# Hybrid attention and feed-forward trunk on one core: the transpositions of the probabilities move inside the projection's matmuls

## What is computed

```python
for layer in range(DEPTH):                      # DEPTH = 2
    hn = rms_norm(h, norm_mix_g[layer])
    h = h + hybrid_mixer(hn, positions, w_in[layer], ..., w_out[layer], layer)
    hn = rms_norm(h, norm_ffn_g[layer])
    h = h + conv_glu_ffn(hn, w_up[layer], conv_ffn_w[layer], w_down[layer])
return rms_norm(h, final_g)
```

```python
a = softmax(q1 @ k1.T) - lam * softmax(q2 @ k2.T)     # causal, per block of 128 queries
o = a @ v                                             # then rms_norm over the head
```

## Time and profile before

| | |
|---|---|
| median of 3 runs | 2609.04 us (2607.76 to 2612.22) |
| the profiled execution | 2612.52 us, of which 2610.7 us are the span of its instructions |
| TensorE busy in the span | 2437.4 us (93%) |
| VectorE, ScalarE, GpSimd busy | 1522.6, 880.9 and 1192.4 us |
| attention with projections, first layer | about 84 to 459 us of the span |
| the same in the second layer | about 1364 to 1739 us |

### The profile page before, as it was taken

One profiled execution on the slowest core, in us unless ns is written; L12 is line 12 of the kernel. 1 busy time (PEld: TensorE's weight loads), 2 busy tenths in 40 slices (PEclk: granted clock), 3 DMA queues, 4 the chain that ended last, 5 costly groups with the idle time before them and its releaser, 6 DMA issues.

```text
span 2610.7 us, 30963 instructions
## 1 busy us (share of the span) xinstructions
PE 2437.4 (93%) x11478; PEld 2017.6 (77%) x11478; DVE 1522.6 (58%) x2161; ACT 880.9 (34%) x1667; POOL 1192.4 (46%) x786
## 2 busy tenths in 40 slices
PE   7799999797999999999989999979889999999996
PEld 6688888675788888888768888868658888888884
DVE  8544777637545555555575456774565555555546
ACT  3344444413322333332414344443232332222322
POOL 3111221347666666666421121131676666666663
PEclk9899999898999999999989999989989999999997
DMA  3000101320111111111210010112111111111111
GB/s 141 25 25 25 33 28 38 92 57 25 49 49 65 49 49 49 54 60 62 95 66 25 25 33 25 33 49 60 57 33 49 58 56 65 49 49 49 49 49 65
DMA packets 55749, 131.33 MB, mean 50 GB/s; under 512 B 4784, under 2 KB 24368, under 8 KB 55600
## 3 DMA queue, kind: packets, MB, share of 16 engines
q1 hardware_dynamic: 54016, 128.07, 15.0%
q10 hardware_dynamic: 1584, 1.28, 0.2%
HBM read 119.64 MB, written 9.44 MB: 49 GB/s over the span
## 4 chain that ended last, share of the span: by engine, by line
PE 69%; DVE 20%; ACT 4%; issue 3%; POOL 3%; DMA 1%; DVEq 0%; POOLq 0%; SPq 0%; ACTq 0%
PE ps L780 14%; PE ps L781 13%; PE ps L782 13%; PE ps L747 6%; PE ps L749 6%; PE ps L748 6%; PE ps L988 3%; DVE k_next L1790 3%; PE ps L975 2%; DVE h L1471 2%; PE ps L962 1%; PE ps L963 1%; ACT prob L1233 1%; DVE q_next L1446 1%; DVE h L1469 1%
## 5 line engine op out<-in xcount | busy, mean ns | idle before, releaser
L539 POOL CAST w_hi<-stage 128x1024 fp32r<-128x1024 f32 x68 | 70.7, 1040 | 859.4 <-PE ps L749 796.7
L747 PE MATMUL ps<-x_hi,w_hi 128*128 128x512 f32 x960 | 389.3, 406 | 11.3 <-POOLq L544 4.7
L574 POOL TENSOR_TENSOR w_lo<-more_stage,w_hi 128x512 fp32r<-128x512 f32 x202 | 293.7, 1454 | 209.8 <-ACT w_hi L1302 192.4
L574 POOL TENSOR_TENSOR w_lo<-stage,w_hi 128x512 fp32r<-128x512 f32 x194 | 281.4, 1451 | 214.2 <-ACT w_hi L1302 197.9
L749 PE MATMUL ps<-x_hi,w_lo 128*128 128x512 f32 x960 | 377.7, 393 | 0.0
L748 PE MATMUL ps<-x_lo,w_hi 128*128 128x512 f32 x960 | 376.7, 392 | 0.0
L1408 DVE TENSOR_TENSOR h<-ps,h 128x1024 f32<-128x1024 f32 x160 | 194.4, 1224 | 192.3 <-PE ps L782 189.0
L780 PE MATMUL ps<-T_hi,w_hi 128*128 128x512 f32 x704 | 282.0, 401 | 19.7 <-DVE T_lo L1674 6.5
L780 PE MATMUL ps<-mix,w_hi 128*128 128x512 f32 x704 | 279.3, 397 | 10.9 <-POOLq L577 5.8
L781 PE MATMUL ps<-T_lo,w_hi 128*128 128x512 f32 x704 | 279.6, 397 | 0.0
L782 PE MATMUL ps<-T_hi,w_lo 128*128 128x512 f32 x704 | 279.3, 397 | 0.0
(11 more groups left out here) (200 smaller groups left out, 4582.7 us busy)
## 6 DMA issues: line engine op xcount, KB each, us to landing
stage<-stream SPq DMA_DIRECT2D x112, 512.0 KB, 3.7
more_stage<-stream SPq DMA_DIRECT2D x68, 512.0 KB, 4.3
h<-x_t SPq DMA_DIRECT2D x16, 512.0 KB, 5.5
stage<-stream SPq DMA_DIRECT2D x18, 448.0 KB, 4.6
saved_h<-h SPq DMA_DIRECT2D x8, 512.0 KB, 4.8
h<-saved_h SPq DMA_DIRECT2D x8, 512.0 KB, 3.3
out_t<-h SPq DMA_DIRECT2D x16, 256.0 KB, 2.1
stage<-stream SPq DMA_DIRECT2D x18, 64.0 KB, 4.8
```

Source lines behind the costliest of these rows:

```text
L574: pool.tensor_tensor(block_of(w_lo, n), raw, block_of(w_hi, n).bitcast(f32), ALU.subtract)\
L747: pe.matmul(out, w_hi[:, s, w], hi, start=start, stop=False)
```

## The change

In units 0 to 4 the turn of the first group (with `turn_v` in step 0) is no longer issued ahead of the half projection but inside it, behind its third row (key 3 of `between`). The turn of the second group, where a step has one, is issued ahead of the eighth and last row (key 7) and no longer behind the projection. Unit 5 keeps its order. No instruction is added or taken away, and no other engine's list is touched.

```diff
                         if i < QB - 1:
                             scores(g + 1, i + 1)
-                        turn_group(g, i, dilated, layer, u, 0)
-                        if i == 0:
-
-                            pe.wait_ge(evac_done, first_half + PROJECTED_V[u])
-                            turn_v()
+
+                        def turn_first():
+                            turn_group(g, i, dilated, layer, u, 0)
+                            if i == 0:
+
+                                pe.wait_ge(evac_done, first_half + PROJECTED_V[u])
+                                turn_v()
+
+                        def turn_second():
+                            if len(todo) > 1:
+                                turn_group(g, i, dilated, layer, u, 1)
+
                         if u < FINAL:
                             if i % 2 == 0:
                                 n = next_tile()
-                            project_half(n, i % 2, PROJ + i % 2)
-                        elif i >= 2:
+                            project_half(n, i % 2, PROJ + i % 2, {3: turn_first, 7: turn_second})
+                        else:
+                            turn_first()
+                        if u == FINAL and i >= 2:
...
                         for m in range(len(todo)):
-                            if m + 1 < len(todo):
+                            if m + 1 < len(todo) and (m or u == FINAL):
                                 turn_group(g, i, dilated, layer, u, m + 1)
                             ended = attend_group(g, i, dilated, layer, u, m)
```

## The result

The changed kernel took 2617.4 us (median of 7 runs, 2612.88 to 2619.64), the kernel before 2610.53 us beside it (7 runs, 2607.76 to 2612.5). The ratio, estimated from all these runs, is 1.0022 (some 5.7 us), with a 95% interval of 1.0013 to 1.0032; the medians are 6.9 us apart. The kernel is slower by 0.2%, where I had forecast 0.4 us. 2617.4 us lies inside the range given, by 0.6 us. One of e1's twelve executions took 12132.71 us and is left out of every number here.

What follows compares the result with a forecast made beforehand. TensorE was taken as the bound, busy 93% of the span, standing 14 us a layer in the attention. The terms summed to +0.2 us a layer, +0.4 in all: 2609.4 us, range 2602 to 2618.

Steps and rivals of the forecast that it cites:

- Interleaving costs nothing: Half projection on TensorE: a turn moved inside it keeps its 0.11 us a transposition, with a surcharge of 0.
- The first rival: Each of 136 turns moved inside the projection costs 0.11 us, +15.0 us, 2624; decides from 0.04 us each; chance 0.10.
- The five T0 waits go: Step 3 of units 2 to 4, step 0 of units 3 and 4: waits for the softmaxes' difference vanish, -5.9 us a layer.
- Step 6 pays: Step 6 of units 0 to 4: ScalarE's later copies make TensorE wait, 0.98 us in five units, +4.9 us a layer.
- The rotation comes 0.14 later in three places: Step 3 of units 2 to 4: VectorE's rotation, and with it step 4's 0.99 us wait, comes later, +0.4 us a layer.
- the heads 0.2: Step 0 of unit 4: with 1.54 us gone, `turn_heads` comes before the normed heads are there, about +0.2 us.
- T1 earlier: T1 ahead of the last row: small copy waits of units 0 and 1 go, -0.4; later projection ends cost +1.0 us a layer.
- at about 2.8 us: Unit 5's first T0: its 2.40 us wait grows by 0.44, as unit 4's step 7 ends later by T1.
- The sum: -5.9 + 4.9 - 0.4 + 1.0 + 0.6 = +0.2 us a layer, +0.4 us in all, 2609.4 us.
- The split holding VectorE: Rival in step 3: the difference slips behind GpSimd's split and waits up to 2.4 us; +14 us, 2624; chance 0.04.

Runs made afterwards that it cites:

- e1: The changed kernel again, no edit, for a second profile and a narrower interval; 2617.20 us, ratio 1.0019 to the kernel before.
- e2: Against the changed kernel, T1 goes back behind the projection, so only T0 is moved; 2610.28 us, ratio 0.9998 to the kernel before.
- e5: Against the kernel before, T0 late only in step 3 of units 2 to 4 and step 0 of units 3 and 4; 2597.45 us, ratio 0.9950.
- e9: e5 plus T1 behind row 4, copied ahead of the exponentials, in step 4 (units 2 to 4) and step 2 (units 0, 1); 2594.11 us, 0.9931.
- e4: The changed kernel with T0 of step 6 back ahead of the projection; 2596.85 us, ratio 0.9950 to the kernel before.
- e6: The changed kernel with ScalarE's q instructions of step 6 issued behind the copy of T1; 2608.61 us, ratio 0.9992 to the kernel before.
- e7: Against the changed kernel, T0 behind row 2 instead of the third row, and T1 behind the projection; 2605.27 us, ratio 0.9976 to the kernel before.
- e3: Against the changed kernel, T0 goes back ahead of the projection, so only T1 is moved; 2616.41 us, ratio 1.0020 to the kernel before.
- e12: The changed kernel with T1 of unit 4's step 7 back behind the projection; 2614.91 us, ratio 1.0017 to the kernel before.

## Why the prediction was right in its mechanism and short in its sum

The time came out inside the range, and in part by luck. The forecast was +0.4 us and the sum's own range ended at 2614. Of some 7 us between the profiles, the attention has 3.7, and 3.0 lie in a stretch that the prediction didn't mention.

**Interleaving costs nothing: right, nearly.** In e2 a transposition inside the projection takes 0.11 us, as in the earlier trace rows, and whole steps leave room for under 0.02 us a turn, which is half of the 0.04 from which the rival would decide. e5 and e9 move turns inside too and are faster by what their waits say. The first rival is out.

**The five T0 waits go: right, a little more than forecast.** From step to step in e2, step 3 of units 2 to 4 became 1.26 to 1.32 us shorter, step 0 of units 3 and 4 1.08 and 1.61. That is 6.5 us a layer against the forecast's 5.9; e5 measured 6.9 and 6.0. I had added up brackets, and as at A1 above a wait costs 0.1 to 0.2 us more than its bracket says.

**Step 6 pays: right, but too small.** The prediction's "new wait of 0.98 us", five times, is there to 0.01 us from start to start, and e4, e6 and e7 show its cause and its size from three sides. But a place costs more: 1.10 us each by e4 and, over steps 6 and 7 of e2, 1.12 (plain) and 1.21 (dilated). Of this 0.10 is A1's slower spacing behind the wait, and in e2 some 0.1 is the passage from products to wide matmuls in step 7. The sum had neither.

**The rotation comes 0.14 later in three places, +0.4, and the heads 0.2: wrong.** The wait of A1 in step 4 stays at 0.99 us in the changed kernel, and ahead of `turn_heads` it shows no wait:

```profile
289.27 0.49 PE L988 MATMUL ps<-v_cur,padded 128*128 128x128 f32 x2 [0.99 <-ACT padded L1201]
```

**T1 earlier, -0.4 + 1.0: the step that failed.** I counted 0.6 us a layer; e3, which does this alone, lost 1.6 and 2.3, and the changed kernel less e2 (T1's move, with T0 late) 1.7 and 2.2. The pieces, from the changed kernel's distances less e2's and from the waits: units 0 and 1 lose 1.2 us in both layers from unit 0's step 1 on, where I had +0.2 for the two units (unit 0's step 0 gives back 0.5 in the first layer and nothing in the second). The largest single one is A1 in step 2 of unit 1, which waits 1.12 us where it waited 0.64. The passages from unit 3 to 4 and from 4 to 5 lose 0.45 each, where I had 0.44 for the second alone: there the next scores wait for the row maxima, 0.41 and 0.22 us by their brackets. In step 0 of unit 3, T0's wait grows from 0.90 to 1.37 us in e3, which the changed kernel hides behind its three rows. The first of these two in the timeline of the changed kernel:

```profile
388.03 0.39 PE L962 MATMUL ps<-k_twice,q_split 128*128 128x256 f32 x1 [0.41 <-DVE neg_top L1514]
```

These are the scores of step 1, which wait for the maxima of the unit's first scores. Before, T1 with its four blocks (0.44 us) lay between the two and covered this wait. The prediction named the late end of the projection as a cost, but priced it at places with a known wait. It put +0.44 on unit 5's first T0, "at about 2.8 us". The loss came at that passage, 0.45 us, and e12, which puts that T1 back, wins it back; but T0's wait measured 2.39, so it lies ahead of T0. The prediction didn't ask which waits of zero would become positive.

**The sum.** T0's move: forecast -5.9 + 4.9 + 0.6 = -0.4 us a layer, measured -0.2 (e2). That it fits so well is luck: -6.5 from the T0 waits, +5.8 from steps 6 and 7, +0.7 spread over the other steps. T1's move: forecast +0.6, measured about +2. Attention: forecast +0.4 us for both layers, measured +3.7.

**The split holding VectorE: didn't come.** VectorE's timeline in step 3 of the changed kernel, and then GpSimd's:

```profile
278.38 0.89 DVE L1531 SCALAR_TENSOR_TENSOR prob<-prob,factor 128x640 f32<-128x640 f32 x1
279.18 0.68 DVE L1397 TENSOR_TENSOR k_next<-ps,rstd_all 128x512 f32<-128x512 f32 x1
...
281.30 2.49 DVE L1480 TENSOR_TENSOR h<-h,sin_t 128x1024 f32<-128x1024 f32 x1
```

```profile
279.20 1.04 POOL L539 CAST w_hi<-stage 128x1024 fp32r<-128x1024 f32 x1 [11.89 <-PE ps L749]
280.31 2.40 POOL L541 TENSOR_TENSOR w_lo<-stage,w_hi 128x1024 fp32r<-128x1024 f32 x1
```

The difference began 0.8 us ahead of GpSimd's cast and 1.9 ahead of the split, and took 0.89 us as in the earlier trace rows; the rotation's long operation was slow before and is so now (2.61 and 2.49 us).

**Outside the attention: half found, and its cause open.** Between 568 and 580 us the granted clock is 1.00 in all three profiles of the kernel before and 0.86 in all three of the changed one. At the same place of the second layer it fell in one of three and in two of three. The row of the kernel before for that window, and that of e1 (the changed kernel):

```profile
568.00:580.00 12.00, 10.15 (x45) 7.93 (x43) 3.00 (x5) 1.23 (x2) 8.30 (x5) 1.00 0.48 147
```

```profile
568.00:580.00 12.00, 10.17 (x38) 7.96 (x37) 0.69 (x1) 0.65 (x2) 10.32 (x5) 0.86 0.29 76
```

In nearly the same busy time TensorE began 38 matmuls and not 45. 0.86 over 12 us is up to 1.7 us lost. So up to 1.7 of the middle stretch's +3.0 us are this fall, and behind the second attention one fall more in three left no difference. The fall isn't the only place. The stretch from one attention to the next took 886.1, 883.8 and 883.1 us in the kernel before and 887.1, 887.5 and 887.4 in the changed one. It took 883.2 and 883.3 in e2 and e4, but 888.1 to 888.4 in e5, e6 and e9, whose attention is shorter. The clock's record has the lower level for 33 us of it in the third profile of the kernel before, e2 and e4, for 44 and 50 in the other two of the kernel before, and for 47 to 55 in all others. So the stretch has a short and a long form, the kernel before shows both, and much of the +3.0 is how often each came. The same spread is in the medians: e9's five executions are 2587.14 us and four of 2593.93 to 2595.75. But none of these counts makes the change their cause. The experiments don't sort by the fall: e5 and e6 show the fall in one layer, e3, e7, e9 and e12 in both, e2 and e4 in none. The one path that I could name, unit 5's later start, e12 tried: with the last T1 back behind its projection the clock fell just the same. What decides whether it falls there stays open, and with it whether these 3 us belong to the change. The 3.7 us of the attention do.

## What to carry to other kernels

A moved step wins only where it waited: T0 moved in the five steps of a layer that waited was worth 13 us in the two layers (e5), moved in all forty nothing (e2). Before moving a producer later, read the consumer engine's list behind it, with its slack, and move nothing where the slack is smaller than the delay: here 0.93 against 2.06 us, and 1.1 us lost each time. And for a step moved earlier, ask which waits of zero its old place covered; then look for the opposite move, a short copy put into time in which its engine stands anyway, which gave the best kernel here (e9, 0.9931).

## What the runs showed of the hardware

Transpositions of 128x128 in float32 stood between matmuls of 128x512 at 0.11 us each, ahead of the projection and inside it alike; the 40 moved T0 of a layer cost under 0.02 us each on top (e2). Nine wide matmuls right behind narrow products took 2.17 us, 0.12 more than behind the scores (e2, steps 7 and 6). TensorE lost 1.08 us by a wait whose bracket says 0.81 (e4 against the changed kernel). Executions of one program differ where nothing in it does: the first scores start up to 2.6 us apart, and one wait of TensorE for VectorE, at 606 and 1886 us in the kernel before, is 7.4 us in four of that kernel's six passages and 5.9 in two. In the 11 profiles of the other kernels it is always 5.9; why is open. A single span can't tell 3 us here; distances between two places of the program can tell 0.5, and 0.1 behind unit 0's step 0. And the granted clock falls between its two levels (2.4 and 1.2 GHz) at one place, from 568 to 580 us, in some executions of a kernel and not in others, to a mean of 0.86. TensorE's busy time in that window is 10.15 us where it stayed and 10.17 where it fell, with 45 and 38 matmuls.
